# A decoder block with recurrence, feed-forward and experts: eight modulation chunks moved from the recurrence to the feed-forward block

## What is computed

```python
mod = jax.nn.silu(c) @ w_ada[layer] + b_ada[layer]          # 1024 x 6144
sh1, sc1, g1, sh2, sc2, g2 = jnp.split(mod, 6, axis=-1)
h = modulate(x, sh1, sc1)
...
x = x + g1[:, None, :] * mix
h = modulate(x, sh2, sc2)
x = x + g2[:, None, :] * hier_moe(h, ...)
```

## Time and profile before

| what | value |
|---|---|
| median of 3 runs | 1145.15 us (1139.17 to 1148.46) |
| the profiled execution's own time | 1143.86 us |
| its span, first to last instruction | 1142.1 us |
| mean granted TensorE clock | 0.989 of full |
| TensorE busy | 1063.0 us, 93% |
| VectorE, ScalarE busy | 462.3 us, 353.9 us |
| moved by DMA | 316.31 MB, 277 GB/s |

### The profile page before, as it was taken

The page is one execution under the profiler, slowest core; times in us unless marked ns, Lnnn a source line. Parts: engine busy times, 40 slices in busy tenths (PEclk is TensorE's granted clock), DMA queues, the critical chain, the costliest instruction groups (busy, mean ns, idle before and its releaser), DMA issues.

```text
span 1142.1 us, 17887 instructions
## 1 busy us (share of the span) xinstructions
PE 1063.0 (93%) x7545; PEld 722.8 (63%) x7545; DVE 462.3 (40%) x698; ACT 353.9 (31%) x508; POOL 39.6 (3%) x32
## 2 busy tenths in 40 slices
PE   5999989899999999998999999999899989898986
PEld 4996767789879999886987453434244433242432
DVE  4784244365663534457649261212122212121212
ACT  5742312273454443446543230101011111010102
POOL 0002200000200010000000000000000000000000
PEclk9999999899999999999989999999999999999999
DMA  9454366415645554645465969999999999999994
GB/s 317 157 196 162 105 224 224 150 74 182 205 139 176 188 182 148 239 167 177 147 216 192 371 244 422 420 420 420 421 420 422 421 420 421 420 422 420 420 420 191
DMA packets 95061, 316.31 MB, mean 277 GB/s; under 512 B 7878, under 2 KB 32790, under 8 KB 70294
## 3 DMA queue, kind: packets, MB, share of 16 engines
q1 hardware_dynamic: 93958, 312.70, 71.2%
q10 hardware_dynamic: 1040, 2.69, 0.7%
HBM read 314.32 MB, written 1.05 MB: 276 GB/s over the span
## 4 chain that ended last, share of the span: by engine, by line
PE 71%; DMA 20%; DVE 4%; ACT 2%; issue 2%; SPq 0%; POOL 0%; DVEq 0%; ACTq 0%
DMA arena<-in_w 20%; PE bank L1458 11%; PE bank L751 11%; PE bank L752 11%; PE bank L753 11%; PE bank L1482 4%; PE bank L737 4%; PE bank L1002 3%; PE bank L917 2%; PE bank L1438 1%; PE bank L951 1%; PE bank L728 1%; PE bank L1495 1%; PE bank L698 1%; DVE arena L2544 1%
## 5 line engine op out<-in xcount | busy, mean ns | idle before, releaser
L1458 PE MATMUL bank<-ring,hT 128*64 128x512 f32 x512 | 226.9, 595 | 30.0 <-DMA arena<-in_w 28.8
L1458 PE MATMUL bank<-arena,hT 128*64 128x512 f32 x512 | 226.9, 595 | 0.0
L753 PE MATMUL bank<-h_high,ring_low 128*128 128x256 f32 x688 | 193.5, 281 | 0.0
L1458 PEld LDWEIGHTS bank<-ring,hT 128*64 128x64 f32 x512 | 67.8, 137 | 182.3 <-issue 130.2
L548 DVE TENSOR_TENSOR ring_low<-ring,hi_high 128x2048 fp32r<-128x2048 f32 (+2 forms) x58 | 126.1, 2219 | 102.8 <-ACT hi_high L1629 102.7
L751 PE MATMUL bank<-h_high,hi_high 128*128 128x256 f32 x528 | 150.2, 284 | 0.7 <-DVE h_low L2134 0.7
L752 PE MATMUL bank<-h_low,hi_high 128*128 128x256 f32 x528 | 149.2, 283 | 0.0
L1629 ACT ACTIVATE hi_high<-ring 128x2048 fp32r<-128x2048 f32 (+2 forms) x58 | 104.5, 1855 | 94.4 <-DMA ring<-in_w_ffn_up 35.5
L753 PEld LDWEIGHTS bank<-h_high,ring_low 128*128 128x128 f32 x688 | 130.8, 190 | 0.0
L1482 PE MATMUL bank<-arena 128*64 128x512 f32 x384 | 113.3, 595 | 7.1 <-DVE hT L2756 6.7
L2762 DVE TENSOR_TENSOR arena<-arena,bank 128x512 f32<-128x512 f32 x16 | 17.3, 1084 | 231.1 <-ACT arena L1986 231.1
(11 more groups left out here) (401 smaller groups left out, 1712.7 us busy)
## 6 DMA issues: line engine op xcount, KB each, us to landing
arena<-in_w SPq DMA_DIRECT2D x112, 1024.0 KB, 23.0
ring<-in_w SPq DMA_DIRECT2D x80, 1024.0 KB, 20.5
ring<-in_w_in SPq DMA_DIRECT2D x15, 2048.0 KB, 7.9
ring<-in_w_ada SPq DMA_DIRECT2D x12, 2048.0 KB, 9.2
ring<-in_w_ffn_gate SPq DMA_DIRECT2D x11, 1024.0 KB, 5.5
ring<-in_w_ffn_up SPq DMA_DIRECT2D x11, 1024.0 KB, 8.2
ring<-in_w_ffn_down SPq DMA_DIRECT2D x5, 2048.0 KB, 7.9
ring<-in_w_o SPq DMA_DIRECT2D x2, 2048.0 KB, 7.8
```

The lines of the kernel that those rows point to most:

```text
L753: return mm(ps, a[1], b[0], start=False, stop=stop)
L1458: last = mm(both(6 + half, x), hg[:, k, (2 * q + x) * CAP:(2 * q + x + 1) * CAP], w13s[x][k // 4][:, k % 4, half * EF:(half + 1) * EF], st ...
```

## The change

The list of loads no longer holds the eight chunks. Each is loaded by SP in two halves of 1 MB (four of the eight k blocks each) into the place of `xn1`, the normed input of the feed-forward block, which is no longer read once it is transposed. The turns move into the feed-forward loop: the two halves of chunk t are multiplied behind f = 2t+2 and f = 2t+3 (`ada_part`), the sum of chunk t-1 comes behind f = 2t+2. SP issues half 0 of a chunk behind load ff t+3 when the former chunk's products are done, and half 1 when half 0 is used. ScalarE's row copies stand at the top of the even steps. Two filler products take the place of turn 0 in the attention. Small parameter loads hang on other keys.

```diff
-    o += [("o", 0), ("o", 1)] + ada_banks(0) + [("o", 2), ("o", 3)]
+    o += [("o", p) for p in range(PAIRS)]
...
-    o += [("ff", m) for m in range(KF)]
+    for f in range(KF):
+        t = f // 2 - 1
+        o += [("ff", f)] + ([("as", ADA_EARLY[t - 1])] if f % 2 == 0 and 0 < t <= len(ADA_EARLY) else [])
+        o += [("ad", ADA_EARLY[t])] if f % 2 == 0 and 0 <= t < len(ADA_EARLY) else []
...
-        modp = {c: (junk[:, 512 * (c % 2):512 * (c % 2) + 512] if c in ADA_LATE else B("modp", 2)[:, c % 2])
-                for c in ADA_EARLY + ADA_LATE}
+        modp = {c: junk[:, 512 * (c % 2):512 * (c % 2) + 512] for c in ADA_EARLY + ADA_LATE}
+        ada_half = B("xn1").rearrange("p (k c) -> p k c", k=KD // 2)
...
-        for c in ADA_EARLY:
-            modulation(c)
         for c in range(1, 4):
             gate_columns(c)
...
# SP, in the loop over the loads
-                if key == ("ada", 3):
+                if key == ("gate", 2):
...
+                if key[0] == "ff" and 3 <= key[1] < 3 + len(ADA_EARLY):
+                    c = ADA_EARLY[key[1] - 3]
+                    src = cols(A["w_ada_2"][0], c * 512, c * 512 + 512)
+                    if key[1] == 3:
+                        drained(sp, ("hT", 1, 3))
+                    else:
+                        filled(sp, ("ad", ADA_EARLY[key[1] - 4]))
+                    sp.dma_start(ada_half, src[:, 0:4, :]).then_inc(S("half_full"), 16)
+                    sp.wait_ge(S("half_used"), key[1] - 2)
+                    sp.dma_start(ada_half, src[:, 4:8, :]).then_inc(S("half_full"), 16)
-                if key == ("ada", 0):
+                if key == ("gate", 1):
...
# TensorE
+            def ada_part(t, part):
+
+                c = ADA_EARLY[t]
+                pe.wait_ge(S("half_full"), 16 * (2 * t + part + 1))
+                if part == 0:
+                    pe.wait_ge(S("cb"), 1)
+                    ps = write(pe, ("ad", c))
+                else:
+                    ps = bank[BANK["ad", c][0]]
+                for j in range(4):
+                    last = mm(ps[32 * j:32 * j + 32, 0:512], cb[:, 4 * part + j, :], ada_half[:, j, :], start=(part == 0),
+                              stop=(part == 1), skip_group_check=True)
+                if part == 0:
+                    last.then_inc(S("half_used"), 1)
+                else:
+                    last.then_inc(*full(("ad", c)))
...
                 if p == 2:
-                    ada(0)
+                    keep_busy(write(pe, ("o", p)), 2)
...
-            ada(1)
...
-                ada(lv + 1)
...
-            ada(LEVELS + 1)
...
-            ada(LEVELS + 2)
...
                 last.then_inc(*full(("ff", f)))
+                t = f // 2 - 1
+                if f % 2 == 0 and 0 < t <= len(ADA_EARLY):
+                    ada_sum(ADA_EARLY[t - 1])
+                if 0 <= t < len(ADA_EARLY):
+                    ada_part(t, f % 2)
...
# ScalarE
             for f in range(KF):
+                if f % 2 == 0 and 0 < f // 2 - 1 <= len(ADA_EARLY):
+                    ada_rows(ADA_EARLY[f // 2 - 2])
                 ps = filled(act, ("ff", f))
...
# VectorE
                 V.tensor_tensor(fT[:, f, :], sil[:, f % 2, :], ps[:, SEQ:2 * SEQ], ALU.mult).then_inc(*free(("ff", f)))
+                if f % 2 == 0 and 0 < f // 2 - 1 <= len(ADA_EARLY):
+                    ada_sum(ADA_EARLY[f // 2 - 2])
                 if f % 2:
                     low_parts(N_FF + f // 2 + 3)
```

More of the change, by code:

```diff
@@ L165 @@
 PARCOL, PARBLOCK = par_columns()
-def ada_banks(turn):
-    return ([("as", ADA_EARLY[turn - 1])] if turn else []) + ([("ad", ADA_EARLY[turn])] if turn < len(ADA_EARLY) else [])
 def plan_banks():
@@ L186, in plan_banks @@
     o += [("tok", 1, a) for a in range(4)]
-    o += [("o", 0), ("o", 1)] + ada_banks(0) + [("o", 2), ("o", 3)]
+    o += [("o", p) for p in range(PAIRS)]
     both = [(i, q) for i in range(NT) for q in range(2)]
-    o += [("g", i, q, e) for i, q in both for e in range(2)] + ada_banks(1)
+    o += [("g", i, q, e) for i, q in both for e in range(2)]
     o += [("n", i, q) for i, q in both]
     for lv in range(1, LEVELS):
-        o += [("x", i, lv, q) for i, q in both] + ada_banks(lv + 1)
+        o += [("x", i, lv, q) for i, q in both]
         for i, q in both:
             o += ([("d", i, lv, q)] if lv < LEVELS - 1 else []) + [("dt", i, lv, q)]
-    o += [("w1", i, q) for i, q in both] + ada_banks(LEVELS + 1)
-    o += [("u", i, q) for i, q in both] + ada_banks(LEVELS + 2)
+    o += [("w1", i, q) for i, q in both]
+    o += [("u", i, q) for i, q in both]
     o += [("ry", 0, c) for c in range(2)] + [("psi", 0), ("psi", 1), ("phi", 1)]
@@ L248 @@
     ("zb", NT * HEADS * P, TOKENS, WKV),
-    ("modp", 2 * 512, TOKENS, GATES), ("gm", NT * HEADS * 4 * CH, WKV, WKV), ("dd", NT * HEADS * CH, WKV, WKV),
+    ("gm", NT * HEADS * 4 * CH, WKV, WKV), ("dd", NT * HEADS * CH, WKV, WKV),
     ("ddT", NT * HEADS * CH, WKV, WKV), ("xx", NT * HEADS * CH, WKV, WKV), ("up", NT * HEADS * DH, WKV, WKV),
@@ L292 @@
     "g1": 25600, "lw": 25600, "gtmp": 26112, "g2": 26624, "lvlf": 26624, "junk": 27648, "bon": 27648, "fin": 27648,
-    "osb": 28672, "kk": 28672, "fpost": 28672, "ysq": 28672, "one": 28672, "acT": 29184, "modp": 29696, "xn1": 29696,
+    "osb": 28672, "kk": 28672, "fpost": 28672, "ysq": 28672, "one": 28672, "acT": 29184, "xn1": 29696,
     "xn2": 29696, "ew2_4": 30208, "kT": 30720, "tk": 20480, "orw": 30720, "ry": 31232, "sil": 31744, "cb": 32256,
@@ L1745, in _ @@
             for p in range(PAIRS):
-                if p == 2:
-                    ada_rows(0)
                 ps = filled(act, ("o", p))
@@ L1754, in four @@
                 return ps[:, 0:4 * w].rearrange("p (h t) -> p h t", h=4)
-            ada_rows(ADA_EARLY[1])
             for lv in range(1, LEVELS):
@@ L1760, in _ @@
                     A_(xx[:, i, 4 * q:4 * q + 4, :], four(ps, CH), ACT.Copy).then_inc(*free(("x", i, lv, q)))
-                ada_rows(ADA_EARLY[lv + 1])
             for i, q in both:
@@ L1764, in _ @@
                 A_(zb[:, i, 4 * q:4 * q + 4, 0:DH], four(ps, CH), ACT.Copy).then_inc(*free(("w1", i, q)))
-            ada_rows(ADA_EARLY[LEVELS + 1])
             for i, q in both:
@@ L2313, in _ @@
                                     ALU.mult).then_inc(*free(("g", i, q, e)))
-            ada_sum(ADA_EARLY[0])
             dve.wait_ge(S("eye"), 2)
@@ L2323, in _ @@
             for lv in range(1, LEVELS):
-                ada_sum(ADA_EARLY[lv])
                 for i, q in both:
@@ L2331, in _ @@
                     V.copy_predicated(ddT[:, i, hs, :], lmask(lv, 1), four(ps)).then_inc(*free(("dt", i, lv, q)))
-            ada_sum(ADA_EARLY[LEVELS])
-            ada_sum(ADA_EARLY[LEVELS + 1])
             def ry_out(i):
@@ L2366, in _ @@
             state_out(2)
-            for c in (2, 3):
-                drained(dve, ("as", c))
-            V.tensor_scalar(modc[:, 8:16], modc[:, 8:16], 1.0, None, ALU.add).then_inc(S("mod"), 1)
             for i in range(NT):
@@ L2435, in _ @@
                 V.tensor_tensor(fT[:, f, :], sil[:, f % 2, :], ps[:, SEQ:2 * SEQ], ALU.mult).then_inc(*free(("ff", f)))
+                if f % 2 == 0 and 0 < f // 2 - 1 <= len(ADA_EARLY):
+                    ada_sum(ADA_EARLY[f // 2 - 2])
                 if f % 2:
                     low_parts(N_FF + f // 2 + 3)
+            for c in (2, 3):
+                drained(dve, ("as", c))
+            V.tensor_scalar(modc[:, 8:16], modc[:, 8:16], 1.0, None, ALU.add).then_inc(S("mod"), 1)
             for n in range(N_FF + KF // 2 + 3, BY_TWO):
```

## The result

The changed kernel takes 1208.41 us (median of 4 runs, 1207.54 to 1210.57) against 1146.81 for the kernel before, run beside it on the same chip: 1.055 times as long, 95% interval 1.050 to 1.0605. The forecast was 1212. The profiled execution took 1210.57 us.

The account below looks back on a forecast made before the run. TensorE was taken to bound the kernel, busy for 93% of the span. Recurrence -28, feed-forward block +76 and clock +20 made +68 on the profiled 1143.9 us: 1212 us, range 1186 to 1238.

Parts of the forecast that it names:

- The loop in the feed-forward block: Feed-forward block: slot free, load, split, copy, sum, half, f makes turns of 21.0 us instead of 11.5; block +76 us in all.
- rival C: Feed-forward block: half 1 isn't hidden, 2 us more each turn, 1228 us; chance 0.08.
- t = 8: Last chunk's turn in the feed-forward block: 1 MB load in after 4.8 us, wait 0.7, +2.7 us in all.
- The clock: Feed-forward block: eight waits each followed by a stretch at half clock, 2.5 us each, +20 us, bounds 0 and 46.
- rival A: Feed-forward block: the waits come but the clock holds, 1192 us; chance 0.20.
- Rival B: Feed-forward block: clock stays low through sum, half and whole f behind each wait, 46 us instead of 20, 1238; chance 0.14.
- The recurrence: Removing the chunks from the recurrence returns 28 us, bounds 5 and 33: products 22.9 plus stalls 5.
- The products' term: Recurrence: chunk products and sums removed from TensorE's chain, 23.8 us less 0.9 not returned at one turn, 22.9 us.
- the stall term: Recurrence: "issue" stalls and low clock may go with the eight 2 MB loads, between nothing and 10 us, taken at 5.
- The fear that denser small products let the clock sink: Recurrence: small products, denser without chunks, might run at half clock, costing up to 18 us.
- Rival D: Feed-forward block: row copies are in time and only the work moves, 1139 us, no difference; chance 0.04.
- T: Feed-forward block: moment the second product of a pair of f steps (f = 2t+1) ends; SP then issues load ff t+3.

Follow-up runs that it names:

- kernel 1: Changed kernel with ScalarE copying a chunk's rows at odd f, ahead of splitting the next load; 1186.62 us, ratio 1.038 to the kernel before.
- kernel 2: Changed kernel with SP issuing half 0 ahead of gate and up of load ff t+3, ScalarE's order kept; 1227.2 us, ratio 1.0736.
- kernel 11: Changed kernel with the splits one pair of steps later, row copies still behind a split; 1188.23 us, ratio 1.0387.
- 3: Changed kernel with both edits: row copy ahead of the split, and half 0 issued ahead of load ff t+3; 1147.52 us, ratio 1.0028.
- kernel 4: Changed kernel with seven filler products on TensorE ahead of each sum and six ahead of the first half 0; 1200.13 us, ratio 1.0501.
- kernel 5: Changed kernel with the eight chunks left out altogether (products, sums, copies, loads); 1114.99 us, ratio 0.9743.
- 8: Changed kernel with rows copied ahead of the split and SP issuing gate, half 0, up, half 1; 1145.76 us, ratio 1.0013.
- 9: Kernel 8 with splits one pair of steps later and SP issuing gate, half 0, half 1, up; 1149.51 us, ratio 1.0045.
- 10: Kernel 8 with the splits one pair of steps later, its order of loads kept; 1145.53 us, ratio 1.0006.
- kernel 7: Kernel before, with chunk products in the recurrence reading constants and the eight chunk loads left out; 1131.63 us, ratio 0.9887.
- kernel 6: Kernel 5 plus the eight 2 MB chunk loads spread over the recurrence, read by nothing; 1134.88 us, ratio 0.9912.

## Why the prediction came out right

**The loop in the feed-forward block: right.** Waits were 50.4 us (23.6 + 21.3 + 5.5) against 52.8 forecast. The seven turns from t = 1 took 23.45 us on average, against 21.0 + 2.5. In these seven turns the waits were 41.8 us against 46.2; that the loads reached the split 8.6 us after their issue and not 9.0 makes 2.8 of the difference. Half 1 was hidden, so rival C didn't come. Kernels 1, 2 and 11 each change one link of the loop (order, landing, which landing), and each time came out as the loop gives it, within the range expected.

**t = 8: mis-sized.** Its wait was 3.1 us and not 0.7. The single 1 MB load took 7.4 us from issue to landing; before, the same transfer took 4.8. Half 1 of the last chunk, issued 6.3 us earlier (482.92), had landed by 488.2, before this load was issued at 489.22. In kernels 1 to 4 and 11, with the same neighbour, the same load took 4.8 to 6.4 us. What made it 7.4 here stays open; the price is 2.4 us.

**The clock: right in mechanism, near in size.** From the start of each sum to the end of its turn TensorE took 1.9 to 3.2 us longer than the same work takes at the full clock, 21.6 over eight turns; forecast 20. Kernel 4, which fills the gaps, puts it at 14 to 19. The eight gaps of 5.5 to 6.7 us (t = 0 to 7) were each followed by a stretch at 1.2 GHz; the ninth, of 3.1 us, was not (1.00 in the last window above). The length of a gap alone doesn't tell which it will be: all eight gaps of kernel 1, seven of them 3.2 to 4.3 us long, were followed by half clock, and so was one of 2.1 in kernel 11. So rival A (1192, the clock holds) was wrong. Rival B too: the half clock ended inside the following f step (at 343.9 in the turn shown), at most 10 us after its begin. The rule of the Trainium skill (TensorE: Matmul & The Clock Gate, "HAM oscillation — how this bites in real kernels") agrees with the trace for eight of the nine waits: what came next ran at the low rate (a first half in 1.93 us instead of 1.06).

**The recurrence: near in sum, wrong in its parts.** -28 was forecast and -32.0 came; in the nine other kernels with this recurrence (1 to 5 and 8 to 11) the FFN starts 28.4 to 30.6 us earlier than before, so -32.0 is the far end. The products' term was 22.9 and kernel 7 gives 20.7. The failing step is the reading of the 15.7 us of L917: they hold the chunk that ran at half the clock, 3.54 instead of 1.85, so 1.7 us of clock were counted as work. The same 1.7 us are missing from the bound of the stall term, which was taken at 5 of at most 10 and is 11.4 by kernel 7: 6.9 of stalls, 3.2 and 1.7 of clock make 11.8. Taking the middle was a guess, and nearly the whole came. The fear that denser small products let the clock sink did not come true; it read 1.00. Its price was too low as well: 76 records pass in 2 us at the full clock, not 67, which makes up to 27 us and not 18.

**The total: partly luck.** By the profiled executions the span grew by 66.7 us, against +68. The recurrence returned 4.0 more than forecast, the block cost 97.2 instead of 96, and 1.6 came behind it; these offset each other in part. The medians, taken side by side, differ by only 61.6.

**Rival D, incomplete.** It said that with ScalarE's copy in time only the work moves: 1139. Kernel 1 does that and took 1187. The prediction called half 0 hidden because it is wanted at T + 14.3, but that date was itself set by the wait; once the copy is in time half 0 is wanted at T + 7.7 and lands nearly 4 us later (30.4 over 8). The cover of the one transfer was the other's lateness. With both cured (3, 8, 10) the kernel is back at the time of before, no faster: the some 30 us that the recurrence gives (kernel 5) are spent again on 2.9 us of work for each of eight chunks, 23 in all, and on some 6 of halves that arrive late. No version with the chunks is measurably faster than the kernel before. One without any late half wasn't reached: half 0 ahead of the load makes half 1 late (3), the gate part ahead makes half 0 late (8, 9, 10). With one buffer of 1 MB for the halves a turn of 14.4 us must hold two landings one after the other, beside 2 MB for the f steps; whether a second buffer would cure it wasn't tested.

## What to carry to other kernels

Before moving work beside a stage that loads through a ring, write the loop that the move closes (slot free, load, split, copy, product, slot free) in the order of each engine's queue: a short copy queued behind a step that waits for a load inherits the whole landing. When a wait hides a second transfer, curing the first alone returns only part (here 22 of 61.6 us), so look at what is late next before pricing a cure. And price a wait on the bounding engine with what its clock loses behind it, here about 40% on top (21.6 on 50.4 us).

## What the runs showed of the hardware

- Loads that TensorE doesn't use still slow it. With dense small products beside 2 MB loads it stood 15.7 us for nothing that the profile shows, then ran at half the clock, once for over 12 us (kernel 6, 0.50 in all of 206 to 218 us); without the loads these stalls sum to some 2 us (kernel 5) or 0.5 (kernel 7). In this execution, from 143 to 210 us, the DMA queues (packets, MB, share) were:

```profile
q1 hardware_dynamic: 8674, 16.80, 70.4%
q8 instruction: 12, 0.20, 1.2%
```

  So instructions come through the same DMA engines as the loads, in pieces of 16 KB. The stalls are late instructions, by their places: counted in products and weight loads of TensorE, the eight stalls of kernel 6 are 255, 257, 511, 513, 256, 512 and 255 apart, all multiples of 256 within one, and those of the kernel before 255, 257, 511, 768 and 768. Each of the eight ended 2.2 to 2.6 us after a piece of the instruction queue had started (at 169.40 for the one that ended at 171.79). What holds such a piece up beside the loads isn't shown: once started it takes 0.9 to 1.4 us with loads and without. No run changes the instructions alone.
- A 2 MB load reached ScalarE 8.3 to 9.8 us after its issue in the kernels before and after, and 10.7 to 11.0 with 1 MB just ahead of it in the same queue (kernel 2, the seven turns).
- With TensorE kept busy by fillers the same loads of ff t+3 took 0.7 us longer on average (kernel 4). Not explained.
